# Output projection of a hybrid encoder layer: plain 16 tiles against Strassen's seven half-size products

## The reference

```python
y = jnp.concatenate([ya, yb, yc], axis=-1)               # (1, 1024, 2048)
return x + jnp.einsum('bse,ed->bsd', y, w_out)           # w_out (2048, 2048), float32
...
return rmsnorm(x, final_gain)                            # over the 2048 columns of each frame
```

## Time and profile before

| | us |
|---|---|
| median of 3 runs (1933.59 to 1935.51) | 1933.65 |
| the profiled execution, its own time | 1934.78 |
| its span, first to last instruction | 1932.9 |
| PE busy in the span | 1894.5 (98%) |
| DVE, ACT, POOL busy | 747.6, 380.2, 944.4 |

### The profile page before, as it was taken

One profiled execution on the slowest core, in us unless ns is written; L12 is line 12 of the kernel. 1 busy time (PEld: TensorE's weight loads), 2 busy tenths in 40 slices (PEclk: granted clock), 3 DMA queues, 4 the chain that ended last, 5 costly groups with the idle time before them and its releaser, 6 DMA issues.

```text
span 1932.9 us, 24836 instructions
## 1 busy us (share of the span) xinstructions
PE 1894.5 (98%) x9310; PEld 1576.2 (82%) x9310; DVE 747.6 (39%) x929; ACT 380.2 (20%) x465; POOL 944.4 (49%) x907
## 2 busy tenths in 40 slices
PE   7899999999999999999999999999999999999996
PEld 6688888888888888888888888888888888888884
DVE  7856747475657512213132313332232261111115
ACT  7313122122222101102020202221121240000001
POOL 6645444454545444444435344454554546555551
PEclk9999999999999999999999999999999999999998
DMA  7111111110111111111101111211111245111114
GB/s 242 45 39 49 39 49 43 38 54 33 54 38 54 38 59 41 56 44 50 49 33 61 38 61 39 74 52 40 62 52 43 100 159 222 49 49 49 48 48 176
DMA packets 59532, 124.19 MB, mean 64 GB/s; under 512 B 7130, under 2 KB 7903, under 8 KB 59492
## 3 DMA queue, kind: packets, MB, share of 16 engines
q1 hardware_dynamic: 51130, 96.12, 14.5%
q10 hardware_dynamic: 8362, 27.48, 3.9%
HBM read 107.31 MB, written 16.27 MB: 64 GB/s over the span
## 4 chain that ended last, share of the span: by engine, by line
PE 90%; DVE 5%; ACT 2%; issue 1%; DMA 1%; POOL 0%; SPq 0%; ACTq 0%; DVEq 0%; POOLq 0%
PE prj L366 74%; PE prj L392 2%; PE mix L474 2%; PE mix L546 2%; PE mix L529 2%; PE mix L430 1%; PE prj L414 1%; PE mix L539 1%; ACT arena L720 1%; DVE arena L1339 1%; PE mix L469 1%; PE mix L501 1%; PE mix L441 0%; PE mix L504 0%; PE mix L490 0%
## 5 line engine op out<-in xcount | busy, mean ns | idle before, releaser
L366 PE MATMUL prj<-mv_hi,w_hi 128*128 128x512 f32 x2240 | 703.3, 395 | 0.5 <-issue 0.2
L366 PE MATMUL prj<-mv_lo,w_hi 128*128 128x512 f32 x2240 | 692.1, 390 | 0.0
L366 PE MATMUL prj<-mv_hi,w_lo 128*128 128x512 f32 x2240 | 690.8, 390 | 0.0
L337 POOL TENSOR_TENSOR pool_pad<-eps_sb 128x1 f32<-128x1 f32 x300 | 82.8, 276 | 923.2 <-PE prj L366 878.9
L366 PEld LDWEIGHTS prj<-mv_hi,w_lo 128*128 128x128 f32 x2240 | 420.8, 188 | 89.0
L366 PEld LDWEIGHTS prj<-mv_lo,w_hi 128*128 128x128 f32 x2240 | 420.7, 188 | 88.6
L366 PEld LDWEIGHTS prj<-mv_hi,w_hi 128*128 128x128 f32 x2240 | 411.5, 188 | 81.2 <-issue 2.4
L338 POOL TENSOR_SCALAR w_hi<-w_raw 128x512 fp32r<-128x512 f32 x300 | 470.2, 1567 | 0.0
L341 POOL TENSOR_TENSOR w_lo<-w_raw,w_hi 128x512 fp32r<-128x512 f32 x300 | 402.6, 1342 | 25.0
L720 ACT ACTIVATE arena<-arena 128x1024 f32<-128x1024 f32 (+1 forms) x121 | 124.2, 1036 | 380.5 <-DVE arena L1055 166.6
L972 DVE TENSOR_TENSOR arena<-prj,rstd 128x1024 f32<-128x1024 f32 x59 | 72.0, 1220 | 173.9 <-PE prj L366 173.9
(11 more groups left out here) (131 smaller groups left out, 1457.9 us busy)
## 6 DMA issues: line engine op xcount, KB each, us to landing
w_raw<-in_w SPq DMA_DIRECT2D x300, 256.0 KB, 3.1
arena<-in_xT SPq DMA_DIRECT2D x16, 512.0 KB, 4.7
arena<-in_xT ACTq DMA_DIRECT2D x16, 512.0 KB, 13.2
outT<-arena SPq DMA_DIRECT2D x32, 256.0 KB, 2.6
y_scratch<-arena ACTq DMA_DIRECT2D x15, 512.0 KB
arena<-y_scratch ACTq DMA_DIRECT2D x15, 512.0 KB, 5.0
arena<-rel_scratch ACTq DMA_DIRECT2D x5, 320.0 KB, 4.2
arena<-in_rot ACTq DMA_DIRECT2D x2, 512.0 KB, 3.7
```

The costliest lines, as they stand in the source:

```text
L337: nc.gpsimd.tensor_tensor(pool_pad[:], eps_sb[:], eps_sb[:], ALU.mult)
L366: last = nc.tensor.matmul(prj[pair][:, cols], wt[q][:, kk, :], mv[:, k, cols], start=(k == 0 and wt is w_hi and mv is mv_hi), stop=(k == K ...
```

## The change

The output projection `w_out` transposed times `y` (as 2 x 2 blocks: features of the output, features of `y`, frames, all halved) is computed by Strassen's seven products of half size instead of eight. `PRODUCTS` lists for each: the quarters of `w_out` that are added or subtracted, the quarters of `y`, and the quarters of the output to which the product is added, with signs. A product is 8 steps (`PAIRS`), one per pair of output blocks; a step is 8 blocks of a combination of `y` x 3 = 24 matmuls of 128x512 into one PSUM bank, and uses 2 granules of weights. There are 56 steps and 112 granules.

- PE: steps instead of tiles, 1344 matmuls (before 1536), written out, no loop. Steps 0 to 3 are opened together and their last block waits for the last block of `y`. Step `s` waits until step `s-4` has been taken out of its bank. `project_last` is gone.
- DVE: adds or subtracts each step's bank into one or two blocks of the arena (`accumulate`), where the residual has been loaded first; adds the two raw granules of a weight combination (`weight_sum`, from product 2 on); makes the sum and the low part of `y`'s combinations (`comb_add`, `comb_low`); sums squares; scales. All of it in one fixed order per step (a turn `v` of the loop `for v in range(STEPS)`, on DVE as on ACT).
- ACT: high part of each combination of `y` (`comb_high`) and of each granule (`w_high`), squares.
- POOL: only the low parts of granules. The first 8 granules go the old way.
- SP: loads raw granules into 8 buffers (`RAWS`), two for each granule of a two-term product; halves of `y` from `y_scratch` into 4 slots; the residual (32 DMAs of 256 KB); the output. The residual leaves ACT's queue.
- The moving combinations take two slots of 8 half blocks in the lower half of `mv_hi` and `mv_lo`; the upper halves hold the raw granules and the loads of `y`.
- The host lays `w_out` out as `wo`, by pairs and quarters.

The core of the diff:

```diff
+PRODUCTS = [
+    ((A11,), 1, (B12, B22), -1, ((C12, 1), (C22, 1))),
+    ((A22,), 1, (B21, B11), -1, ((C11, 1), (C21, 1))),
+    ((A11, A22), 1, (B11, B22), 1, ((C11, 1), (C22, 1))),
+    ((A21, A22), 1, (B11,), 1, ((C21, 1), (C22, -1))),
+    ((A11, A12), 1, (B22,), 1, ((C12, 1), (C11, -1))),
+    ((A21, A11), -1, (B11, B12), 1, ((C22, 1),)),
+    ((A12, A22), -1, (B21, B22), 1, ((C11, 1),)),
+]
+STEPS = PAIRS * len(PRODUCTS)
+OPEN = 4
+GRANULES = 2 * STEPS
+RAWS = 8
+YSLOTS = 4
...
+        def slot(mv, j, i):
+
+            return mv[:, 4 * (j % 2) + i // 2, half(i % 2)]
+
+        def raw_buf(m):
+
+            return raws[:, m % RAWS, :].rearrange("p (k t) -> p k t", k=GRAN)
+
+        def y_buf(idx, n):
+            return y_in[:, idx % YSLOTS, half(n)]
...
+            return prj[1 - (s // 2) % 2][:, half(s % 2)]
...
+        raw_of, raw_granule = {}, []
+        for n in range(2 * OPEN, GRANULES):
+            terms = PRODUCTS[n // 2 // PAIRS][0]
+            raw_of[n] = [len(raw_granule) + t for t in range(len(terms))]
+            raw_granule += [n] * len(terms)
...
+        def combs_at(v):
+
+            if OPEN <= v < PAIRS:
+                return [2 * (v - OPEN), 2 * (v - OPEN) + 1]
+            return [v] if PAIRS <= v < Y_COMBS else []
...
+            def load_raw(n):
+                j, p = divmod(n // 2, PAIRS)
+                for m, ab in zip(raw_of[n], PRODUCTS[j][0]):
+                    if m >= RAWS:
+                        sp.wait_ge(w_split, W0 + raw_granule[m - RAWS] + 1)
+                    sp.dma_start(raw_buf(m), wo[p, ab, n % 2]).then_inc(raw_in[m % RAWS], 16)
+
+            def load_comb(idx):
+                if idx >= YSLOTS:
+                    sp.wait_ge(comb_lo, HK + idx - YSLOTS + 1)
+                if idx == HK - 1:
+                    sp.wait_ge(y_stored, 16 * (UNITS + 1))
+                for n, (kb, sh) in enumerate(y_terms(idx)):
+                    sp.dma_start(y_buf(idx, n), y_dram[HK * kb + idx % HK][:, half(sh)]
+                                 ).then_inc(ys_in[idx % YSLOTS], 16)
+
+            def load_residual(p, n, arrived):
+                for row in range(2):
+                    sp.dma_start(acc(p, (row, n)), xT[2 * p + row][:, half(n)]).then_inc(arrived[p], 16)
+
+            sp.wait_ge(w_used, NG * (TO - 1) + 3)
+            sp.wait_ge(y_stored, 16 * UNITS)
+            for n in range(2 * OPEN, 2 * OPEN + RAWS):
+                load_raw(n)
+            for idx in range(YSLOTS):
+                load_comb(idx)
+            sp.wait_ge(filled[1], M1_C + C_M1 * C_HEADS)
+            for p in range(OPEN):
+                load_residual(p, 1, x2_in)
+            sp.wait_ge(comb_lo, HK)
+            sp.wait_ge(y_stored, 16 * (UNITS + 1))
+            for p in range(OPEN, PAIRS):
+                load_residual(p, 1, x2_in)
+            for p in range(PAIRS):
+                load_residual(p, 0, x1_in)
+            more_combs = {8: (4, 5), 9: (6, 7)}
+            more_combs.update({s: (s - 2,) for s in range(10, Y_COMBS + 2)})
+            for s in range(PAIRS, STEPS):
+                load_raw(2 * s)
+                load_raw(2 * s + 1)
+                for idx in more_combs.get(s, ()):
+                    load_comb(idx)
...
+            for n in range(2 * OPEN, GRANULES):
+                pool.wait_ge(wo_hi, n + 1 - 2 * OPEN)
+                nc.gpsimd.tensor_tensor(w_lo[n % NG][:], raw_buf(raw_of[n][0]), w_hi[n % NG][:].bitcast(F32),
+                                        ALU.subtract).then_inc(w_split, 1)
...
+            def product(n, s, rows):
+
+                j = s // PAIRS
+                for i in rows:
+                    pe.wait_ge(comb_lo, HK * j + (i + 1 if j == 0 else HK))
+                    for wt, mv in ((w_hi, mv_hi), (w_hi, mv_lo), (w_lo, mv_hi)):
+                        last = nc.tensor.matmul(
+                            bank(s), wt[n % NG][:, i % GRAN, :], slot(mv, j, i),
+                            start=(i == 0 and wt is w_hi and mv is mv_hi),
+                            stop=(i == HK - 1 and wt is w_lo))
+                return last
+
+            def granule(n, s, q):
+                pe.wait_ge(w_split, W0 + n + 1)
+                product(n, s, range(GRAN * q, GRAN * q + GRAN)).then_inc(w_used, 1)
+
+            for p in range(OPEN):
+                pe.wait_ge(tile_evicted, TO - 1 if p < 2 else TO)
+                granule(p, p, 0)
+                if p >= 2:
+                    c_ss(C_HEADS - 1, p - 2)()
+            for p in range(OPEN):
+                pe.wait_ge(w_split, W0 + OPEN + p + 1)
+                product(OPEN + p, p, range(GRAN, HK - 1))
+            for p in range(OPEN):
+                product(OPEN + p, p, [HK - 1]).then_inc(w_used, 1)
...
+            for s in range(OPEN, STEPS):
+                pe.wait_ge(acc_done, s - 3)
+                for q in range(2):
+                    granule(2 * s + q, s, q)
+                if s == STEPS - 6:
+                    output_ss(1)
+            output_ss(0)
...
+            def comb_high(idx):
+                act.wait_ge(comb_sum, HK + idx + 1)
+                if len(y_terms(idx)) == 2:
+                    src = mix[0][:, half(idx % 2)]
+                else:
+                    src = y_buf(idx, 0)
+                act.wait_ge(w_used, step_used(PAIRS * (idx // HK) - 1) if idx >= HK else W0 - NG + 2)
+                nc.scalar.activation(slot(mv_hi, idx // HK + 1, idx % HK), src, ACT.Copy).then_inc(comb_hi, 1)
+
+            def w_high(n):
+                if two_terms(n):
+                    act.wait_ge(wsum_done, n - first_sum + 1)
+                else:
+                    act.wait_ge(raw_in[raw_of[n][0] % RAWS], raw_count(raw_of[n][0]))
+                act.wait_ge(w_used, W0 + n + 1 - NG)
+                nc.scalar.activation(w_hi[n % NG][:], raw_buf(raw_of[n][0]), ACT.Copy).then_inc(wo_hi, 1)
+
+            def square(q):
+                v, p, c = squares[q]
+                act.wait_ge(acc_done, v)
+                if q >= 2:
+                    act.wait_ge(fsq_added, q - 1)
+                nc.scalar.activation(rstd[:, half(q % 2)], acc(p, c), ACT.Square).then_inc(fsq_ready, 1)
+
+            def final_rms(n, done):
+                act.wait_ge(fss_ready, done + 1)
+                inv_rms(mix[0][:, half(n)], mix[0][:, half(n)], D_MODEL,
+                        (fin_log, 1, done + 1)).then_inc(fin_rstd, 1)
+
+            for v in range(STEPS):
+                for idx in combs_at(v):
+                    comb_high(idx)
+                if OPEN <= v + 2 < STEPS:
+                    w_high(2 * v + 4)
+                    w_high(2 * v + 5)
+                for q, sq in enumerate(squares):
+                    if sq[0] == v:
+                        square(q)
+                if v == STEPS - 5:
...
+            def weight_sum(n):
+                a, b = raw_of[n]
+                for m in (a, b):
+                    dve.wait_ge(raw_in[m % RAWS], raw_count(m))
+                sign = PRODUCTS[n // 2 // PAIRS][1]
+                tt(raw_buf(a), raw_buf(a), raw_buf(b), ALU.add if sign > 0 else ALU.subtract
+                   ).then_inc(wsum_done, 1)
+
+            def comb_add(idx):
+                dve.wait_ge(ys_in[idx % YSLOTS], y_count(idx))
+                if idx >= 2:
+                    dve.wait_ge(comb_lo, HK + idx - 1)
+                if len(y_terms(idx)) == 2:
+                    sign = PRODUCTS[idx // HK + 1][3]
+                    tt(mix[0][:, half(idx % 2)], y_buf(idx, 0), y_buf(idx, 1),
+                       ALU.add if sign > 0 else ALU.subtract).then_inc(comb_sum, 1)
+                else:
+                    nc.vector.memset(wait_pad[:], 0.0).then_inc(comb_sum, 1)
+
+            def comb_low(idx):
+                dve.wait_ge(comb_hi, HK + idx + 1)
+                src = mix[0][:, half(idx % 2)] if len(y_terms(idx)) == 2 else y_buf(idx, 0)
+                hi, lo = slot(mv_hi, idx // HK + 1, idx % HK), slot(mv_lo, idx // HK + 1, idx % HK)
+                tt(lo, src, hi.bitcast(F32), ALU.subtract).then_inc(comb_lo, 1)
+
+            def accumulate(s):
+                j, p = divmod(s, PAIRS)
+                dve.wait_ge(w_used, step_used(s))
+                if j < 2:
+                    arrived = (x2_in, x1_in)[j]
+                    dve.wait_ge(arrived[p], 32)
+                else:
+                    dve.wait_ge(acc_done, s - PAIRS + 1)
+                updates = PRODUCTS[j][4]
+                for c, sign in updates:
+                    last = tt(acc(p, c), acc(p, c), bank(s), ALU.add if sign > 0 else ALU.subtract)
+                last.then_inc(acc_done, 1)
...
+            for v in range(STEPS):
+                if PAIRS <= v + 3 < STEPS and two_terms(2 * v + 6):
+                    weight_sum(2 * v + 6)
+                    weight_sum(2 * v + 7)
+                for idx in combs_at(v):
+                    comb_add(idx)
+                add_squares_of(v - 1)
+                for idx in combs_at(v):
```

(31 more changed lines are left out.)

277 lines of the change are left out of this document (126 added, 151 removed).

## The result

The changed kernel takes **2056.79 us** (median of 4 runs, 2053.47 to 2058.63), the kernel before, beside it on the same chip, 1934.58 us (1933.59 to 1936.31). The ratio is **1.063**, 95% interval 1.061 to 1.065: slower by 122 us, where 84 were forecast, and 1.8 us beyond the upper end of the range.

The account below looks back on a forecast made before the run. PE bounds the kernel before; after the change, a ring of waits among SP, DVE, ACT and POOL. Span 1932.9 - 43.5 + 115 + 4 + 8 + 1.5 = 2017.9, own time about 2018 us; range 1970 to 2055.

Parts of the forecast that it names:

- What is removed: Output projection on PE: 1536 matmuls become 1344, 192 fewer at 0.2268 us each, -43.5 us.
- The ring: Turns 14 to 47: loads, DVE sums, ACT high parts and POOL splits wait in a loop, 8.5 or 9.1 us each, +115 us.
- load: landing 3.1 after issue: In each ring turn: second raw load issued 0.46 after the first, landing 3.1 after issue, 3.56 us together.
- The bound of 3.8 us: Ring's upper case: load landing after 3.8 us, plus a port wait of 1.1; turns 10.9 and 10.3 us, +176.
- The opening: Steps 0 to 3: PE needs the last `y` block after about 20 us, which just fits; +4 us (0 to 8).
- the residual: Loads for step 8 and combinations 4 to 7 stand behind SP's residual DMAs, landing near 1607; +8 us (3 to 12).
- what lies behind turn 47: End of the ring and PE's last 8 steps: no extra cost, since `w_high` runs ahead without combinations.
- The tail: After PE's last matmul: the last norm stands behind one more accumulation on DVE, +1.5 us (0 to 4).
- The port: Every POOL split stops DVE for its whole length, a step takes 7.4 us; about 1970; chance 0.09.
- The ring has slack: Landing, split and handoffs fit under 5.44 us, so all is hidden; about 1898, faster; chance 0.07.
- The clock: PE's granted clock stays low through the 34 turns, steps of 10.9 us, +186; about 2090; chance 0.06.
- What would show it: Steps 18 to 47 of 8.5 to 9.1 us, PE waiting for POOL, DVE for raw DMAs, PE busy about 1850 us.

Follow-up runs that it names:

- experiment 2: Twelve raw slots in place of 8, against the changed kernel; order on DVE unchanged: 1908.42 us, ratio 0.986.
- the best version here: Changed kernel with twelve raw slots, 16 residual loads moved later, first residual loads earlier, two norm sums later on PE: 1899.56 us, ratio 0.9814.
- Experiment 1: Changed kernel with `comb_add` moved ahead of the two weight sums in DVE's turn: 1951.33 us, ratio 1.0075.
- 8: Ten raw slots in place of 8, against the changed kernel: 1965.44 us, ratio 1.0158.
- (4): Changed kernel with only the first of two raw quarters loaded for two-term granules, all sums and splits kept: 1995.64 us, ratio 1.0311.
- (5): Changed kernel with SP waiting for DVE's `comb_add` before issuing `y` loads from step 14 on: 2043.89 us, ratio 1.0561.

## Why the prediction was right in kind and short in size

**What is removed** held: 192 matmuls fewer, and in experiment 2, where nothing else binds, a step is 5.44 us. A kernel that gave all of it back would take 1934.6 - 43.5 = 1891; the best version here, at 1899.6, is 8.5 us from it.

**The ring** is the mechanism. Experiment 1 opens it at the order on DVE, experiments 2 and 8 at the slots, and each takes time away by the turns that it shortens. The step that failed is its term "load: landing 3.1 after issue". From the high part in turn 13 (1653.22) to that in turn 47 the 34 turns took 333.4 us, where 299.8 had been forecast:

| turns | forecast | measured | miss |
|---|---|---|---|
| 16, one-term `y` | 8.5 | 9.31 | 13.0 |
| 18, two-term `y` | 9.1 | 10.25 | 20.6 |

From issue to sum it took 4.42 us in the mean with one-term `y` and 4.82 with two. Over the 34 turns that is 52 us more than forecast, of which the other terms, 4.89 and 5.42 in place of 5.4 and 6.0, gave back 19.

The median row of the kernel before was taken over loads that were not issued four together, and I had argued for it by the rate: 1.5 MB in 9 us is far from what the queues carry. But the average over a turn says nothing about a load within it. Two splits end 1.3 us apart, each frees two slots, and SP issues four raw loads within 2 us and a `y` half or two at their tail. The means from issue to sum, one term and two, order the causes: 3.27 and 3.09 us with two raw loads (4), 4.27 and 4.11 with four and no `y` behind them (5), 4.42 and 4.82 in the changed kernel. So the number of raw loads in the burst costs most, and two `y` halves behind it 0.7; single turns scatter by 1 us and more around each mean. The bound of 3.8 us in the prediction came from a load issued with one other, so it was no bound. The other terms were right or high by a little: splits 1.26 in place of 1.34, since nothing disturbed them, handovers of dependent instructions shorter than the sum of whole durations.

**The opening and the residual** were +12 together, and what lies behind turn 47 was taken as free. The stage from 1562.46 to PE's last matmul (2035.68) is 473.2 us against 350.3 - 43.5 = 306.8, a loss of 166.4. The ring's part is 333.4 - 34 x 5.44 = 148.4, which leaves 18.0 for all three. Some 2 of them lie behind turn 47: from its high part to PE's last matmul it takes 49.0 us, in experiment 2 46.8. The time of the last low part of `y`, forecast for 1581 to 1582, was right (it ended near 1582). Not seen were the wait of DVE's first accumulation for the residual (5.6 us), and that `y` for combination 4 came at 1610.8, not 1607.

**The tail** was +1.5 and came out at -1.0: from PE's last matmul to the end 19.1 us, before 20.2.

So, in spans: 33.6 (ring) + 6.0 (opening, residual and what lies behind turn 47) - 2.5 (tail) = 37.1, which is, up to rounding, the whole difference of 36.9 between the forecast 2017.9 and 2054.8.

**The rivals.** *The port* (1970) is out as the bound here: in the ring a weight sum took 693 ns in the mean. Its mechanism is there and shows as soon as the ring opens (1070 ns), hidden. *The ring has slack* (1898) fell for 8 slots, but it describes the kernel with twelve: 1908, and 1900 with the head mended. *The clock* (2090): it did not stay low, yet it dips after every longer wait, and PE's 786 matmuls in the ring were busy 217 us in place of 178. From 1661.77 to 1986.64 no wait of ACT, DVE or POOL for PE stands in the list, and the part of a turn outside the landing keeps its length whatever the clock: so in the ring it lies in time that PE had to spare, as the prediction said. ACT did wait 20 times for PE in the stage, 40.6 us in all, with the high part of a weight, but all of them before or behind that stretch; how much of that was on the path, and owed to the clock, was not separated. In experiment 2 the granted clock is 1.00 through the ring without any edit to PE: the dips follow from its waits.

**What would show it.** Steps were 9.0 to 11.0 us, not 8.5 to 9.1. DVE waited for raw DMAs, as said. PE was not named as waiting for POOL's split: the profile puts its waits down to the accumulation (21 times, up to 3.8 us) and at the starts of products to the low part of `y` (6 times, up to 13.9, where 7 was forecast). PE was busy 1898 us, not 1850, mostly for the clock's reason. It is the low DMA share with DVE waiting for DMA that identifies the ring, more surely than a name beside PE.

## What to carry to other kernels

When a change puts several engines in a cycle through a ring of buffers, compare the length of the cycle with the bound engine's step, and not only the work of each engine. The cycle is opened cheaply at either of two places: an instruction that stands in a queue behind one it does not need (105 us here), or slots enough that the load does not depend on the split just made (148 us for four of 256 KB). Price a load in a cycle by the last landing of all that is issued with it, not by the median of a quiet stage; and once the cycle is open, look at what the freed engines then collide with.

## What the runs showed of the hardware

- Loads of 256 KB issued together delay each other while the mean rate is low. Four within 2 us in place of two put the last one's time from issue to sum from 3.1-3.3 to 4.1-4.3 us, and two `y` halves behind them to 4.8 (means over 16 and 18 turns), at 146 GB/s over the ring. Within one burst it was 259 GB/s at a DMA share of 0.84. Transfers issued later slow those already under way: with `y` moved away the two-term turns from turn 32 on were 0.76 us shorter.
- After PE's wait of 2.07 us at 1567.4 its granted clock was 0.50 from 1571 to 1573, that is 1.2 GHz, with matmuls 0.427 us apart in place of 0.227. From 1574 it was 1.00 again. The earlier trace rows had shown such a fall only after the end of the matmuls.
- A DVE instruction with two SBUF operands that starts well inside a split of POOL (1.30 us) ends 0.54 to 0.56 us after the split, in three kernels the same way (1.80, 1.41 and, in experiment 1, 1.77 us for 0.69). In experiment 2 six `comb_low` that start 0.08 us into a split and read `mix`, which lies in PSUM, took their usual 0.68 us. The meetings there added 0.38 us to the mean weight sum and at most 1.4 us to the ring.
